# Products over 512 columns of two weight units in the openings of the sub-layers

## The reference

```
def swiglu(x, w_gate, w_up, w_down):
    return (jax.nn.silu(x @ w_gate) * (x @ w_up)) @ w_down
...
    for i in range(DEPTH):
        y = swiglu(rms_norm(h, g[0]), ffn_w_gate[i, 0], ffn_w_up[i, 0], ffn_w_down[i, 0])
        h = h + 0.5 * rms_norm(y, g[1])
        u = rms_norm(h, g[2])
        y = nsa_mixer(u, ...) if i % 2 == 0 else fox_mixer(u, ...)
        h = h + rms_norm(y, g[3])
        y = swiglu(rms_norm(h, g[4]), ffn_w_gate[i, 1], ffn_w_up[i, 1], ffn_w_down[i, 1])
        h = h + 0.5 * rms_norm(y, g[5])
```

## Time and profile before

| | us |
|---|---|
| median of 3 runs | 1025.35 |
| lowest and highest | 1025.02, 1028.08 |
| span of the profiled execution | 1022.4 |
| PE busy | 1010.1 (99%) |
| DVE busy | 638.3 (62%) |
| ACT busy | 518.8 (51%) |
| moved by DMA | 189.58 MB, mean 185 GB/s |

### The profile page before, as it was taken

The page is one execution under the profiler, slowest core; times in us unless marked ns, Lnnn a source line. Parts: engine busy times, 40 slices in busy tenths (PEclk is TensorE's granted clock), DMA queues, the critical chain, the costliest instruction groups (busy, mean ns, idle before and its releaser), DMA issues.

```text
span 1022.4 us, 14363 instructions
## 1 busy us (share of the span) xinstructions
PE 1010.1 (99%) x5979; PEld 866.0 (85%) x5979; DVE 638.3 (62%) x761; ACT 518.8 (51%) x712; POOL 119.1 (12%) x213
## 2 busy tenths in 40 slices
PE   8999999999999999999999999999999999999997
PEld 7888888898667998888889888888988689888886
DVE  5656565747686765655576655556548776555654
ACT  5544445644564554454464444445556665454442
POOL 0000000213263300000030000001103320000000
PEclk9999999999999999999999999999999999999999
DMA  9767775577403275565556565655674336655651
GB/s 260 251 205 251 233 236 197 174 226 235 137 1 124 83 247 176 195 195 179 202 166 224 188 202 175 200 193 178 210 254 166 114 103 210 202 183 188 204 174 74
DMA packets 138424, 189.58 MB, mean 185 GB/s; under 512 B 7442, under 2 KB 120439, under 8 KB 138360
## 3 DMA queue, kind: packets, MB, share of 16 engines
q1 hardware_dynamic: 133734, 172.83, 52.2%
q0 software_dynamic: 4480, 15.77, 4.6%
q10 hardware_dynamic: 146, 0.07, 0.0%
HBM read 185.99 MB, written 1.09 MB: 183 GB/s over the span
## 4 chain that ended last, share of the span: by engine, by line
PE 94%; POOL 2%; DVE 2%; DMA 1%; ACT 1%; issue 1%; DVEq 0%; POOLq 0%; ACTq 0%
PE ps L1182 90%; PE ps L1594 2%; PE ps L1407 1%; POOL ms L417 1%; DMA kvN<-kvN 1%; POOL rstd L419 0%; ACT work L556 0%; POOL ms_half L413 0%; DMA res<-in_x 0%; DVE normed L839 0%; DVE res L823 0%; DVE work L936 0%; DVE probT_buf L955 0%; POOL work L450 0%; ACT work L645 0%
## 5 line engine op out<-in xcount | busy, mean ns | idle before, releaser
L782 DVE TENSOR_TENSOR wlo<-raw,whi 128x2048 fp32r<-128x2048 f32 x145 | 332.6, 2294 | 127.8 <-ACT whi L530 127.7
L1182 PE MATMUL ps<-xhl,whi 128*128 128x512 f32 (+1 forms) x1664 | 387.5, 376 | 0.0
L1182 PEld LDWEIGHTS ps<-xhl,whi 128*128 128x128 f32 x1664 | 287.1, 189 | 49.8 <-issue 2.8
L530 ACT ACTIVATE whi<-raw 128x2048 fp32r<-128x2048 f32 x150 | 286.3, 1909 | 27.8 <-DMA raw<-in_fox_w_in 10.4
L1182 PEld LDWEIGHTS ps<-xhl,wlo 128*128 128x128 f32 x1536 | 207.9, 190 | 13.8
L1182 PE MATMUL ps<-xhl,wlo 128*128 128x256 f32 x1536 | 213.1, 282 | 0.0
L1182 PE MATMUL ps<-whi,xhl 128*128 128x256 f32 (+1 forms) x640 | 131.9, 319 | 0.1
L1182 PE MATMUL ps<-whi,hhi 128*128 128x512 f32 x320 | 124.9, 390 | 0.0
L1182 PE MATMUL ps<-wlo,hhi 128*128 128x512 f32 x320 | 124.9, 390 | 0.0
L1182 PE MATMUL ps<-whi,hlo 128*128 128x512 f32 x320 | 124.5, 389 | 0.0
L1182 PEld LDWEIGHTS ps<-whi,xhl 128*128 128x128 f32 x640 | 100.7, 191 | 9.8 <-issue 2.9
(11 more groups left out here) (173 smaller groups left out, 776.4 us busy)
## 6 DMA issues: line engine op xcount, KB each, us to landing
raw<-in_ffn_w_down SPq DMA_DIRECT2D x44, 1024.0 KB, 4.9
raw<-in_ffn_w_gate SPq DMA_DIRECT2D x40, 1024.0 KB, 5.4
raw<-in_ffn_w_up SPq DMA_DIRECT2D x40, 1024.0 KB, 5.4
raw<-in_fox_w_in SPq DMA_DIRECT2D x10, 1024.0 KB, 5.4
raw<-in_nsa_w_in SPq DMA_DIRECT2D x8, 1024.0 KB, 5.5
big<-in_nsa_cmp_w POOLq DMA_DIRECT2D x8, 512.0 KB, 6.5
raw<-in_nsa_w_out SPq DMA_DIRECT2D x4, 1024.0 KB, 5.6
raw<-in_fox_w_out SPq DMA_DIRECT2D x4, 1024.0 KB, 4.9
```

What stands on the lines that cost most here:

```text
L530: nc.scalar.activation(whi[:, u % RING, :], raw_of(u), ACT.Copy).then_inc(w_hi, 1)
L782: nc.vector.tensor_tensor(wlo[:, u % RING, :], raw_of(u), whi[:, u % RING, :].bitcast(F32), ALU.subtract).then_inc(w_lo, 1)
L1182: return nc.tensor.matmul(out_, l, r, start=start, stop=stop)
```

## The change

The two by-token units of an opening stand in neighbouring slots of the ring. The change multiplies them together: a product keeps the same stationary tile of tokens and streams 256 columns from each of the two slots (pair_cols). pair_high has the 16 products by the high weights, pair_low the 8 by the low ones, for a tile of tokens; unit_done rises by 2 at the end of the second tile. A bank of PSUM now holds a tile of tokens of both units instead of both tiles of a unit; first_unit, bank_of and the evacuations read it so. The order of the opening is written anew: high products of the pair, high products of unit 2, low products of the pair, T1's first group, five products of unit 3, T1's second group, and the rest. In fox units 2 and 3 are paired as well on tile 1 and for their low products. twin_features, outside the openings too, waits for w_hi first and for w_lo only ahead of its first low product. The lists of ACT, DVE, POOL and SP keep their order.

```diff
@@ -592,7 +598,7 @@ def silu(f, u0, c):
-                    src = ps[:, GB, :]
+                    src = first_unit(f, 0)
...
@@ -1232,6 +1240,8 @@ def twin_features(u, bank, between=None):
-                pe.wait_ge(w_lo, u + 1)
+                pe.wait_ge(w_hi, u + 1)
...
+                    if a == 0:
+                        pe.wait_ge(w_lo, u + 1)
                     for k in range(KT):
                         last = mm(ps[:, bank + a, 0:S], wl[:, k, cols], xhi[:, k, :], False, k == KT - 1)
...
+            def pair_cols(w, u, k):
+                v = w[:, u % RING, k * UC:(k + 1) * UC]
+                return bass.AP(v.tensor, v.offset, [list(v.ap[0]), [2048 * ((u + 1) % RING - u % RING), 2], [1, UC]])
+            def pair_high(u, bank, t, x_parts=None):
+                tile = slice(t * P, (t + 1) * P)
+                pe.wait_ge(w_hi, u + 2)
+                for k in range(KT):
+                    if x_parts is not None and k in (0, 4):
+                        pe.wait_ge(xlo_ready, x_parts + 1 + k // 4)
+                    for v in (xhi, xlo):
+                        mm(ps[:, bank + t, :].rearrange("p (a n) -> p a n", a=2), v[:, k, tile], pair_cols(whi, u, k), k == 0 and v is xhi, False)
+            def pair_low(u, bank, t):
+                tile = slice(t * P, (t + 1) * P)
+                pe.wait_ge(w_lo, u + 2)
+                for k in range(KT):
+                    last = mm(ps[:, bank + t, :].rearrange("p (a n) -> p a n", a=2), xhi[:, k, tile], pair_cols(wlo, u, k), False, k == KT - 1)
+                if t == TT - 1:
+                    last.then_inc(unit_done, 2)
...
-                tokens(u0, u0 % RING, GB, (0,), 4 * s)
-                tokens_tile(u0 + 1, UB, 0)
-                high(u0 + 2, OB, 0, {12: T1[0], 15: T1[1]})
-                high(u0 + 3, fourth, 0)
-                tokens(u0, u0 % RING, GB, (1,), 4 * s + 2)
-                tokens(u0 + 1, (u0 + 1) % RING, UB, (1,))
-                high(u0 + 2, OB, 1)
+                pair_high(u0, GB, 0, 4 * s)
+                if KINDS[s] == "fox":
+                    tokens_high(u0 + 2, OB, 0, True)
+                    pair_low(u0, GB, 0)
+                    T1[0]()
+                    tokens_high(u0 + 3, OB, 256, False, {5: T1[1]})
+                    pair_high(u0, GB, 1, 4 * s + 2)
+                    pair_low(u0, GB, 1)
+                    pair_high(u0 + 2, OB, 1)
+                    pair_low(u0 + 2, OB, 0)
+                    pair_low(u0 + 2, OB, 1)
+                    return
+                twin_high(u0 + 2, OB, 0)
+                pair_low(u0, GB, 0)
+                T1[0]()
+                twin_high(u0 + 3, YB, 0, {5: T1[1]})
+                pair_high(u0, GB, 1, 4 * s + 2)
+                pair_low(u0, GB, 1)
+                twin_high(u0 + 2, OB, 1)
                 if product_T:
                     product_T()
-                low(u0 + 2, OB)
-                high(u0 + 3, fourth, 1)
-                low(u0 + 3, fourth)
+                twin_low(u0 + 2, OB)
+                twin_high(u0 + 3, YB, 1)
+                twin_low(u0 + 3, YB)
```

More of the change, by code:

```diff
@@ L282, in up_bank, with first_unit @@
             return YB if f and c == 1 else GB
+        def first_unit(f, j):
+            if f == 0:
+                return ps[:, GB + j, :].rearrange("p (a n) -> p a n", a=2)
+            return ps[:, GB:GB + 2, j * UC:(j + 1) * UC]
         def arrival_of(u):
@@ L294, in bank_of @@
             if kind == "nsa":
-                return (GB, UB, OB, YB)[k] if k < 4 else GB + 2 * (1 - k % 2)
-            return GB + k if k < 4 else GB + 2 * (k % 2)
+                return (GB, GB, OB, YB)[k] if k < 4 else GB + 2 * (1 - k % 2)
+            return GB + 2 * (k // 2) if k < 4 else GB + 2 * (k % 2)
         def by_token(kind, k):
@@ L588, in silu @@
                         act.wait_ge(prod_ready, NCH * f)
-                    src = ps[:, GB, :]
+                    src = first_unit(f, 0)
                 else:
                     act.wait_ge(gate_sum, (NCH - 1) * f + c)
-                    src = silu_sb
-                nc.scalar.activation(silu_sb, src, ACT.Silu).then_inc(silu_ready, 1)
+                    src = silu_sb.rearrange("p (a n) -> p a n", a=2)
+                nc.scalar.activation(silu_sb.rearrange("p (a n) -> p a n", a=2), src, ACT.Silu).then_inc(silu_ready, 1)
             def hidden_hi(f, u0, c):
@@ L692, in evacuate @@
                                 act.wait_ge(w_lo, u0 + 3)
-                            src = ps[:, bank, :].rearrange("p (a n) -> p a n", a=2)
+                            src = ps[:, bank:bank + 2, (k % 2) * UC:(k % 2 + 1) * UC]
                             dst = vN[:, k] if kind == "nsa" else vF[:, :, k * UC:(k + 1) * UC]
@@ L859, in product @@
                     dve.wait_ge(unit_done, u0 + 2)
-                    up_ = ps[:, UB, :]
+                    up_ = first_unit(f, 1)
                 else:
@@ L865, in product @@
                     dve.wait_ge(up_sum, (NCH - 1) * f + c)
-                    up_ = up_sb
+                    up_ = v
                 dve.wait_ge(silu_ready, NCH * f + c + 1)
@@ L869, in product @@
                     dve.wait_ge(hlo_ready, NCH * f + c)
-                nc.vector.tensor_tensor(prod_sb, silu_sb, up_, ALU.mult).then_inc(prod_ready, 1)
+                prod_, silu_ = (w.rearrange("p (a n) -> p a n", a=2) for w in (prod_sb, silu_sb))
+                nc.vector.tensor_tensor(prod_, silu_, up_, ALU.mult).then_inc(prod_ready, 1)
             def hidden_lo(f, c):
@@ L1262, in twin_low, with tokens_high @@
                 last.then_inc(unit_done, 1)
-            def tokens_tile(u, bank, t, before={}):
-                wh, wl = wcols(u % RING)
+            def pair_cols(w, u, k):
+                v = w[:, u % RING, k * UC:(k + 1) * UC]
+                return bass.AP(v.tensor, v.offset, [list(v.ap[0]), [2048 * ((u + 1) % RING - u % RING), 2], [1, UC]])
+            def pair_high(u, bank, t, x_parts=None):
                 tile = slice(t * P, (t + 1) * P)
-                o_ = ps[:, bank, t * UC:(t + 1) * UC]
+                pe.wait_ge(w_hi, u + 2)
[11 more added lines that the diff above has]
+                    last.then_inc(unit_done, 2)
+            def tokens_high(u, bank, c0, first, before={}):
+                wh = wcols(u % RING)[0]
                 n = 0
@@ L1275, in tokens_tile @@
                             before[n]()
-                        mm(o_, v[:, k, tile], wh[:, k, :], n == 0, False)
+                        mm(ps[:, bank, c0:c0 + UC], v[:, k, 0:P], wh[:, k, :], first and n == 0, False)
                         n += 1
[L1278 to L1305, removed]
             def first_tokens():
```

3 lines of the change are left out of this document (removed).

## The result

| | before | changed |
|---|---|---|
| median, us | 1025.53 | 1031.62 |
| lowest and highest, us | 1025.02, 1028.08 | 1028.8, 1031.83 |
| ratio of times | | 1.0052 [1.0037, 1.0067] |
| span of the profiled execution, us | 1022.4 | 1030.0 |

Four executions of each. The changed kernel is slower by 0.5%, between 3.8 and 6.9 us; the forecast was 5.0. From the page of the changed kernel: its busy times, the chain that ended last by engine, and the costliest group of products (busy us, mean ns | idle ahead of it, and what ended most of it).

The account below looks back on a forecast made before the run. PE, busy 99% of the span, was taken as the bound, its time a list of products. Terms: feed-forward +4.8, nsa +0.5, fox -0.3, together +5.0 on 1025.35 us, giving 1030.3; range 1026.8 to 1034.5.

Parts of the forecast that it names:

- The price of a pair: On PE, a product streaming two ring slots costs 0.2265 us, as a contiguous one of 512 columns; at worst 0.240.
- Shorter openings: PE's work in an opening shrinks by 0.80 us in ffn and nsa, 1.23 in fox; product_T still covered.
- The late load: In three feed-forward openings unit 4's load issues 2.08 us later; PE waits 2.4 for gate_add, net +1.6 each, +4.8 together.
- nsa: In nsa's opening gather comes 1.2 us later and PE waits 1.3 for it; net +0.5, bounds -0.8 and +1.3.
- fox: In fox's opening the forget gates start 1.4 us later; PE waits 0.9 for unit 3's evacuation; net -0.3, bounds -1.23, +0.9.
- The relaxed wait at zero: twin_features waiting for w_hi first earns nothing: gate_sum comes last in openings, and PE has no low-weight wait elsewhere; zero.
- The clock: Rival, 8%: PE's clock falls to its lower level behind the feed-forward waits, all three or none, 1.9 us; zero in the sum.

Follow-up runs that it names:

- Gate first: Changed kernel with gate_cross_out and gate_add of chunk 1 moved ahead of unit 4's conversions on ACT and DVE in feed-forward openings; 1021.64 us, ratio 0.9976.
- done together: Kernel before, without pairs, with unit 0 reported done only together with unit 1; 1036.42 us, ratio 1.0122.
- the halves: Changed kernel with only DVE's move (gate_add ahead of unit 4's low part): 1025.34 us, 1.0004; with only ACT's (gate_cross_out ahead of its high part): 1031.67, 1.0065.
- the second profile: Changed kernel run and profiled again without any edit; 1029.14 us, ratio 1.0052 to the kernel before.
- Gate first, low first: Changed kernel with gate_cross_out and gate_add moved ahead of unit 4's conversions, but twin_features waiting for w_lo first as before the change; 1027.77 us, ratio 1.0028.
- openings with fillers: Changed kernel with 18 or 9 dummy identity products ahead of unit 4's gate_sum wait in feed-forward openings; 1035.24 us (1.0106) and 1028.62 us (1.0047).
- 9 fillers: Changed kernel with 9 dummy identity products on PE ahead of unit 4's gate_sum wait in each feed-forward opening; 1028.62 us, ratio 1.0047.

## Why the prediction held, point by point

**The price of a pair** was right. Sixteen products from two slots take 357.84 - 354.19 = 3.65 us, 0.228 each; the median over all of them is 0.227, against 0.2265 taken. The other end, 0.240, is out. The Trainium skill (TensorE: Matmul & The Clock Gate, Back-to-back issue gap) would give N/2.4 + 2.5 ns, 0.216, for isolated products, a condition that the prediction left out, and 0.131 in a sustained stream; the trace agrees with neither.

**Shorter openings** were right: product_T 0.80 us earlier, T1 at 7.46 behind the first product (forecast 7.4). (The time at which chunk 0's product would be ready adds to 360.2, where the prediction has 360.25; nothing hangs on it.) Gate first kept 0.71 to 0.82 of it in each feed-forward stage.

**The late load** was right in each step: issue 2.10 later relative to the opening (forecast 2.08), high part begun 5.46 behind the issue (5.4), gate_add at its end 26.22 behind the opening's start (forecast 369.09 - 342.92 = 26.17). The waits sum to 7.0 in three (forecast 2.4 each), and unit 4 starts 1.67 later (1.6). That it is this mechanism and not the pairs' new order is shown by "done together"; that it goes through the lists of ACT and DVE, and mostly through DVE's, by the halves.

**nsa**: in the changed kernel's DVE and PE timelines, against the earlier trace rows,

```profile
232.14 1.80 DVE L1014 TENSOR_TENSOR flat<-pairs,smallT 128x960 f32<-128x960 f32 x1 [4.88 <-DMA pairs<-work]
...
234.00 3.67 PE L1189 MATMUL ps<-big,flat 128*64 128x256 f32 x32 [1.06 <-DVE flat L1014]
```

Less the 0.15 of the first stage, gather ends 1.18 later (forecast 1.2), PE waits 1.06 (1.3), and the point is reached 0.48 later (0.5). Behind it the wait for kvN is 1.3 instead of 0.9, which the prediction did not have. In the second profile gather came only 0.71 later and nsa lost nothing (-0.05): how early POOL's copies land varies by as much as PE's loss there.

**fox**: DVE and ACT of the changed kernel, against the earlier trace rows:

```profile
749.53 0.47 DVE L1145 TENSOR_SCALAR pairs<-ps,bf 32x256 f32<-32x256 f32 x1
...
752.53 0.57 ACT L701 ACTIVATE big<-ps 128x512 f32<-128x512 f32 x1
```

Fox opens 6.12 later than before; beyond that the gates' step is 1.32 later (forecast 1.4). PE waits 0.6 (0.9), net -0.33 and -0.26 (-0.3).

**The relaxed wait at zero** was right for this kernel and wrong as a judgement: its worth was covered by gate_add. "Gate first, low first" shows that it carries 5.3 us once gate_add is out of the way.

**The clock** is where the prediction was off. It had this as a rival at 8%, all three waits or none, and put it at nothing in its sum. In fact one of three was followed by a fall in both profiles of the changed kernel, and in the four other kernels that kept the wait one or two were; the opening of s=2 had it in all six profiles. Its price was right in kind (1.9 forecast, 1.7 measured), its chance mis-sized. Without the fall the stages sum to +5.9 in the first profile and +4.6 in the second, around the forecast's 5.0. With it they give +7.6 and +6.2, and the runs some 5.3 by the ratio. So the waits were forecast well, and that the total lies so near to 5.0 with a fall in it is in part luck: the spread of the loads, and of the runs, is as large as this term. In these profiles 9 of the 18 waits for gate_add of 2.0 to 2.4 us were followed by a fall, and so was one wait for kvN of 2.53. None of the six openings with fillers had one, nor did any wait of 1.8 us or less after the start. The Trainium skill (the same page, "Why this matters for your kernels") warns of idle gaps over about 3 us, which the prediction held against this rival; here shorter ones were enough. What decides which of two equally long waits is followed by a fall is left open.

## What to carry to other kernels

If two pieces of work are finished together instead of one after the other, whatever waits for the first is released late: look for who waits on that count, and then at what stands behind the waiting step in each engine's list. Here 0.8 us saved at PE released a load 2.1 us later, and two short operations that stood behind it without needing it made PE wait 2.4 us; setting them ahead turned 0.5% slower into 0.2% faster, and the like in the mixers into 0.4%. The same move in the kernel before, which asks for low weights first, cost 0.5%: an order is worth what the waits around it let through. A relaxed wait shows nothing while another wait ends last at the same place: take that one away before calling it worthless.

## What the runs showed of the hardware

- A product that streams two separate runs of 256 columns costs what one of 512 columns in one piece does: 0.227 us (median), with the slots 8 KB apart in each partition (four openings) and 24 KB (third sub-layer, whose units 0 and 1 lie in slots 3 and 0).
- PE's granted clock fell to its lower level behind some idle times of 2.0 to 2.5 us in the middle of dense work, for about 3.4 us, and came back; a fall behind gate_add cost about 1.7 us. In the second profile of the changed kernel the 25 us ahead of it and the 28 us behind it stood at 1.00; its row (columns as above):

```profile
368.50:371.90 3.40, 3.35 (x8) 2.67 (x9) 3.27 (x3) 1.15 (x3) 0.00 (x0) 0.50 0.93 303
```

- At the end of every profile the granted clock is at its lower level for 0.6 to 3.4 us, behind PE's last product; the mean granted clock of a run holds that stretch and cannot be read as a number of falls (0.998 in the profile of "9 fillers", which has none).
- A float32 product of 128 columns (not fp32r) appears as two instructions in the trace, 0.11 us each.
